# Six slots for gathers instead of eight, and two more weight blocks that stay for a layer's second tile

## What is computed

```python
def reference(...):
    h = layer_norm(x, ln_in_g, ln_in_b)
    for i in range(DEPTH):                      # 2 layers
        mix = token_mixers(h, w_in[i], w_out[i], ...)   # proj = h @ w_in: dq dk dv sq sk sv iq ik iw
        h = layer_norm(ALPHA * h + mix, ...)
        r = ALPHA * h + peer_ffn(h, peer_wq[i], peer_subkeys[i], peer_u[i], peer_v[i])
        r = r + sigmoid(r @ ple_wg[i] + ple_bg[i]) * (p[i] @ ple_wp[i])
        h = layer_norm(r, ...)

def peer_ffn(h, w_q, sub_keys, u_tab, v_tab):   # per token: 8 heads x 16 experts
    ...                                         # top 16 of 16384 by product keys -> eidx, weights g
    act = gelu(einsum('thkd,td->thk', u_tab[eidx], xt))
    return einsum('thk,thkd->td', g * act, v_tab[eidx])
```

## Time and profile before

| | us |
|---|---|
| median of 3 runs | 1690.74 |
| lowest and highest | 1689.99, 1691.75 |
| the profiled execution | 1689.92 |
| its span, first to last instruction | 1688.1 |
| busy: TensorE, VectorE, GpSimd, ScalarE | 1254.6, 1070.1, 573.7, 464.2 |

### The profile page before, as it was taken

One profiled execution on the slowest core, in us unless ns is written; L12 is line 12 of the kernel. 1 busy time (PEld: TensorE's weight loads), 2 busy tenths in 40 slices (PEclk: granted clock), 3 DMA queues, 4 the chain that ended last, 5 costly groups with the idle time before them and its releaser, 6 DMA issues.

```text
span 1688.1 us, 17853 instructions
## 1 busy us (share of the span) xinstructions
PE 1254.6 (74%) x6232; PEld 576.2 (34%) x6232; DVE 1070.1 (63%) x2754; ACT 464.2 (27%) x1270; POOL 573.7 (34%) x516
## 2 busy tenths in 40 slices
PE   8978958686787798685766979677766875555556
PEld 6656723231442274132431337232432221001012
DVE  1448679664679764745768694674667877555553
ACT  1323213242223323422222422251122242111112
POOL 0004333334333322343334242343324344444440
PEclk9999978998989999698997989798988997777789
DMA  6769999999999999999999999999999989999992
GB/s 246 289 249 402 421 421 420 421 421 422 421 421 404 416 406 421 421 421 421 421 420 415 405 415 422 421 417 421 421 419 417 372 344 423 421 422 421 422 421 111
DMA packets 93145, 668.26 MB, mean 396 GB/s; under 512 B 10352, under 2 KB 10992, under 8 KB 12288
## 3 DMA queue, kind: packets, MB, share of 16 engines
q0 software_dynamic: 73728, 536.90, 76.9%
q1 hardware_dynamic: 19152, 130.10, 19.1%
q10 hardware_dynamic: 176, 0.13, 0.0%
HBM read 666.04 MB, written 1.05 MB: 395 GB/s over the span
## 4 chain that ended last, share of the span: by engine, by line
DMA 40%; PE 33%; DVE 16%; ACT 4%; issue 3%; POOL 3%; ACTq 0%; POOLq 0%; DVEq 0%
DMA rows<-uv_dram,rows_of 40%; PE acc L1253 12%; PE bank L1042 8%; DVE rows L1002 8%; PE bank L1056 7%; POOL rows L494 3%; ACT dg L666 2%; PE bank L1230 1%; PE bank L1161 1%; PE bank L1032 1%; PE bank L1051 1%; ACT gel L662 1%; PE bank L1153 1%; DVE i L733 0%; DVE i L724 0%
## 5 line engine op out<-in xcount | busy, mean ns | idle before, releaser
L494 POOL DMA_INDIRECT rows<-uv_dram,rows_of x512 | 573.5, 1120 | 1073.4 <-PE acc L1253 856.2
L1002 DVE CUSTOM_DVE_ANT_0 rows<-rows,hx 128x1024 f32<-128x1024 f32 x512 | 620.0, 1223 | 476.7 <-DMA rows<-uv_dram,rows_of 475.1
L1253 PE MATMUL acc<-rows,dg 128*32 128x512 f32 x2048 | 614.6, 730 | 400.9 <-ACT dg L666 400.9
L1253 PEld LDWEIGHTS acc<-rows,dg 128*32 128x32 f32 x2048 | 114.5, 122 | 806.2 <-ACT dg L666 564.7
L662 ACT ACTIVATE gel<-dots 128x2 f32<-128x2 f32 x256 | 51.9, 203 | 894.5 <-DVE dots L1002 894.1
L1042 PEld LDWEIGHTS bank<-xT,wring 128*128 128x128 f32 x2112 | 246.8, 197 | 36.7 <-issue 30.4
L1042 PE MATMUL bank<-xT,wring 128*128 128x128 f32 x2112 | 255.8, 282 | 2.8 <-ACT xT L509 1.1
L1056 PE MATMUL bank<-wring,xT 128*128 128x512 f32 x384 | 173.1, 599 | 1.4 <-ACT xT L509 1.4
L666 ACT ACTIVATE dg<-idg,gel 128x32 f32<-128x32 f32 x512 | 136.6, 314 | 24.6 <-ACT gel L662 1.1
L1056 PEld LDWEIGHTS bank<-wring,xT 128*128 128x128 f32 x384 | 70.7, 190 | 97.6 <-issue 95.6
L662 ACT ACT_TABLE_LOAD x44 | 56.5, 1283 | 0.9
(11 more groups left out here) (156 smaller groups left out, 872.7 us busy)
## 6 DMA issues: line engine op xcount, KB each, us to landing
wring<-wmix_dram SPq DMA_DIRECT2D x96, 1024.0 KB, 9.9
wring<-wclose_dram SPq DMA_DIRECT2D x15, 1024.0 KB, 9.4
rows<-uv_dram,rows_of POOLq DMA_INDIRECT x512, 13.6
rows<-wmix_dram SPq DMA_DIRECT2D x4, 1024.0 KB, 12.7
wring<-wmix_dram SPq DMA_DIRECT2D x4, 512.0 KB, 7.7
rows<-prm_dram SPq DMA_DIRECT2D x2, 1024.0 KB, 10.5
kept<-wmix_dram SPq DMA_DIRECT2D x2, 1024.0 KB, 10.4
fixed<-fixed_dram SPq DMA_DIRECT2D x1, 576.0 KB, 8.3
```

The costliest lines, as they stand in the source:

```text
L494: pool.indirect_dma_start(out=rows[:, slot, :], out_offset=None, in_=uv_d[phase // TILES], in_offset=bass.IndirectOffsetOnAxis(ap=rows_of[ ...
L1002: V.tensor_tensor_reduce(out=rows[:, s, 0:D], in0=rows[:, s, 0:D], in1=hx[:, c, :], scale=1.0, scalar=0.0, op0=ALU.mult, op1=ALU.add, accu ...
L1253: ins = MM(acc[BT * c:BT * c + BT, 512 * i:512 * i + 512], dg[:, s, :], rows[:, s, D + 512 * i:D + 512 * i + 512], start=False, stop=False ...
```

## The change

`RING` goes from 8 to 6, which frees 2 MB of on-chip memory, and `kept` grows from one block to three. The index queries' block and the first values' block are loaded in each layer's first tile, into `kept`, and are not loaded in its second. The extra blocks of the first run lie in slots 2 to 5 of `rows` instead of 4 to 7.

```diff
+STAY = [(U_SK, U_SK + 1), (U_IQ, U_IQ + 1), (U_V, U_V + 1)]
...
-RING = 8
+RING = 6
...
 def loads_of(part, run):
-    if run is CLOSE[3] or (part[:2] == "ps" and (part != "ps0" or run.tile)):
+    if run is CLOSE[3]:
         return []
-    return [b for b in (MIX_BLOCKS if run.stage == "mix" else CLOSE_BLOCKS) if b[0] in units_of(part)]
+    blocks = [b for b in (MIX_BLOCKS if run.stage == "mix" else CLOSE_BLOCKS) if b[0] in units_of(part)]
+    return [b for b in blocks if run.stage == "close" or run.tile == 0 or b not in STAY]
...
-EXTRA_SLOT = 4
+EXTRA_SLOT = 2
...
-            if block[0] == U_SK and run.stage == "mix":
-                place = (KEPT, run.layer)
+            if run.stage == "mix" and block in STAY:
+                place = (KEPT + STAY.index(block), run.layer)
...
     for run in MIX[1::2]:
-        for k in (U_SK, U_SK + 1):
+        for k in [k for block in STAY for k in block]:
             unit[run.key, k] = unit[MIX[run.n - 1].key, k]
...
         rows = sb("rows", [128, RING, 2 * D])
         wring = sb("wring", [128, WRING, 2 * D])
-        kept = sb("kept", [128, 2 * D])
+        kept = sb("kept", [128, len(STAY), 2 * D])
...
-        block_landed = [sem(f"block_landed{i}") for i in range(KEPT + 1)]
+        block_landed = [sem(f"block_landed{i}") for i in range(KEPT + len(STAY))]
...
         def place_of(slot):
-            if slot == KEPT:
-                return kept[:]
+            if slot >= KEPT:
+                return kept[:, slot - KEPT, :]
```

## The result

The changed kernel takes 1792.3 us, the kernel before 1690.8 (median of 4 runs, 1690.0 to 1691.8). Of the changed kernel's four runs (1778.7 to 1806.2) the longest lies 1.5% above the shortest, counts as a slow one, and is left out of the median and the ratio. The ratio is 1.058, 95% interval 1.051 to 1.065: about 100 us more, where 13.4 were forecast, and far outside the range that ended at 1722. The profiled execution took 1792.3 us with a span of 1790.5.

The account below looks back on a forecast made before the run. Saturated DMA engines were taken to bound the kernel. Holes from late gathers, 23.4 us, less 10.0 us for four loads left out, gave 13.4 us more on the median of 1690.74: 1704 us, range 1692 to 1722.

Parts of the forecast that it names:

- What bounds the kernel: From about 126 us, the first gather's issue, nearly the whole time is bytes divided by one rate, 421 GB/s.
- The four loads, 10.0 us: Each layer's second tile skips two 1 MB blocks; four blocks at 2.49 us of saturated DMA time save 10.0 us.
- The method: Per gather: today's landing against the issue of the gather two later plus the shortest reach; no cost if the latter is earlier.
- The reach, 5.8 us: Shortest time from a gather's issue to its landing, read from the very first gather, issued at 126.00 with nothing ahead.
- I put the smooth stretches at nothing: Stretches such as 1400 to 1640 us: no cost from two slots less, with 0.6 us to spare.
- third rival: Ring limits smooth stretches too: reach 1 us longer under load, 25 us on top, 1729 us; chance 0.13.
- The sum of the bursts, 23.4 us: Idle DMA time from late gathers at the start, phase turns and other places; 35.3 us with no help from weights.
- The eight named places: Start 3.3, near 275 us 2.1, gather 82 1.5, second turn 3.6, near 595 us 2.7, third 2.0, gather 326 1.2, last 4.0.
- The start, 3.3 us: First gathers: gather 5 issued at 142.76 lands at 148.6, gather 7 two transfers later at 153.6 instead of 150.3.
- The cover by weights: At bursts, weight blocks under way fill part of the holes: 23.4 us counted instead of 35.3.
- The DMA engines had nothing to do: From 1346 to 1350 us the DMA share is 0.11, read as all eight slots waiting for engines.
- No wait of TensorE for weights, order of loads, blocks that stay: Before 126 us SyncE runs up to two blocks further ahead; TensorE waits for no weights there: no cost, nothing gained.

Follow-up runs that it names:

- The first two experiments: Kernel before with RING = 6 and EXTRA_SLOT = 2, all loads kept: 1802.0 us; kernel before with eight slots, at most six holding a gather: 1793.6 us.

## Why the prediction was wrong

- **What bounds the kernel**: right. Saturated DMA engines, and a ring that has to keep them so.
- **The four loads, 10.0 us**: right, 9 us measured with eight slots.
- **The method** (issue of the gather two later, plus the reach, against today's landing): right in kind. With 7.8 us for the reach it gave seven slots to within a microsecond; for six it falls short by some 13 (below).
- **The reach, 5.8 us, taken as one number for every gather**: this step failed. It was read from the very first gather, which was issued with nothing under way, and for a gather on an empty queue it mostly holds (5.4 to 5.7 us at gathers 5, 78 and 392 of the changed kernel). It was then applied to gathers that are issued behind others in progress. Those with 3 to 5 us to the landing before them landed 7.8 us after their issue and 3.6 us after that landing, where the forecast had 5.8 and 2.5. The forecast called the reach its largest unknown, but the rival that made it 1 us longer had 0.13. A nearer row was in reach: the gather issued at 1353.31, 4.3 us before the landing of the one ahead of it, landed 7.7 us later and 3.5 after that one. The one ahead, issued at 1352.07 with no gather and one weight block in progress, had taken 5.5.
- **"I put the smooth stretches at nothing"**: the largest term that was missing. In the smooth stretch of the kernel before, the first gather of a pair lands by turns some 6.4 and 8.1 us after the issue two later. With 7.8 in place of 5.8 every second pair is 1.4 us late and the others are in time; averaged over both, the reach is 0.5 us per pair too long. Measured: 0.48. In the 240 us of the smooth stretch alone that is 20 us (421 against 386 GB/s). The forecast's third rival had this mechanism, with 25 us on top of the forecast where nearly 90 came.
- **The sum of the bursts, 23.4 us**: mis-sized for the same reason. The eight named places come to 52.6 us in the table above where the forecast has 20.4. The same comparison of the same 254 places with 7.8 us gives about 90 us (each burst once, today's hole in the last turn taken off). Six under way alone cost 103 (the kernel with eight slots and six under way). The 13 us between are open. Two readings were also off: gathers 82 and 326 are 2.1 us late by the forecast's rule, not 2.5.
- **The start, 3.3 us**: the mechanism is in the trace, and so is the failed step. Gather 5 went out at 144.77 and landed 5.7 us later, as forecast; but gather 7, for which two transfers (5.0) had been added, landed 6.4 us after it. From the first issue to gather 7's landing it was 29.8 us, and 24.3 before. What is left of these 5.5 us in the whole time drowns in the spread of the runs.
- **The cover by weights**, for which I took 12 us off: no sign of it. The measured cost lies above the sum without it, with 7.8 us for the reach too.
- **"The DMA engines had nothing to do" from 1346 to 1350 us**: not quite. In the trace of before, 15 of the 16 increments of gather 393 had come by 1347.8, and the last came at 1351.4. The two gathers ahead of it show the same distance, 3.7 us. From about 1347.3 on the share of 0.11 is one 8 KB packet after the other, 0.31 us each: the work of one DMA engine that lagged behind the rest, and not of two.
- **No wait of TensorE for weights, order of loads, blocks that stay**: right. The first two experiments leave nothing for them.

Why the reach behind other gathers is 2 us longer is settled in part. It is not the scattered rows and not the number under way as such. About half of the loss per pair goes away when GpSimd issues direct transfers, and a little more when SyncE does; by what mechanism is open. The increments show that the excess lies in the last of the sixteen parts of a gather, not in the first. Behind a gather in progress the sixteen parts end 2.1 us apart in the changed kernel's smooth stretch (2.75 in that of before), on an empty queue 0.4 to 0.7. DMA engines that have run dry while others still work would fit, and at 1347 us one such case can be seen, but the increments don't name their engine and no run here separates it.

## What to carry to other kernels

A ring's depth is a time, not a count: it has to cover issue to landing under load, plus the work on a slot, plus the issue of all that shares the slot's release. Take the time from issue to landing from a transfer that was issued behind one or two others still in progress. One that starts on an empty queue is too fast for this, whether it is the first of the program (5.8 us here) or stands in the middle of the work (mostly 5.4 to 5.7). And look at GB/s beside the DMA share: here the share stayed at 0.99 while the rate fell by 8%.

## What the runs showed of the hardware

- The share of busy DMA engines does not fall when they begin to starve: 0.99 with 386 GB/s, 1.01 with 421. Packets last longer instead: in the smooth stretch 8 KB packets took 334 ns on average against 314, with a median that was no longer (309 against 313). Of 11,298 packets 294 took more than 0.6 us, up to 2.1, against 13 of 12,343.
- Under the same ring, direct loads by SyncE gave 413 GB/s, by GpSimd 406, and indirect ones by GpSimd 383 to 386.
- A gather issued on an empty queue landed after 5.4 to 5.9 us in most cases (the first one and three of five later ones). One issued 3 to 5 us ahead of the landing before it took 7.8 us on average, and of its sixteen increments the first came after 5.4.
- The matmuls of the two gathers of a pair, which write different parts of `acc`, started within 0.03 us of each other and ended together; a semaphore increment on the last of each arrived 0.06 us apart.
- From eight to seven gathers under way cost 14 us of 1691, from seven to six 88.
